# The first layer's mixer in two token halves, the second placed among the retrieval's slots

## Chip, cores and metric

The kernel runs on one core of one Trainium2 chip. The metric is the device time of one execution in microseconds (us). The kernel before has a median of 3397.39 us in 3 runs (3396.7 to 3400.4).

## What is computed

A decoder trunk of two layers on 512 tokens of 1,024 channels, all in 32-bit floats. Each layer is a mixer and then a channel mixer (PEER), both on normed rows and added to the residual. The first layer's mixer is a gated spatial mixing (gMLP, 4 groups, chunks of 128 tokens) beside an attention of 8 heads with compressed, selected and window branches; since at most 8 blocks of keys exist and the top 16 are asked for, the selected branch sees all causal keys, and so does the window of 512. The second layer's mixer is a gated linear recurrence (HGRN2, 8 heads). PEER takes most of the data:

```python
def even_mixer(h, w_in, ...):
    u, v, q, kc, vc, ks, vs, kw, vw, gt = jnp.split(h @ w_in, EVEN_SPLITS, axis=-1)
    a = chunked_gmlp(jax.nn.gelu(u), jax.nn.gelu(v), a_ln_w, a_ws, a_bs)
    b = nsa(q, kc, vc, ks, vs, kw, vw, gt, cmp_pos, ...)   # o = g0*o_cmp + g1*o_slc + g2*o_win
    return jnp.concatenate([a, b], axis=-1) @ w_out

def peer_block(xb):                       # 128 tokens
    s = scores of xb @ w_q against 2 x 128 keys, 8 heads
    best, pos = top 16 of the 16 x 16 sums of the two top-16 lists
    gate = softmax(best)
    act = gelu(einsum('td,thkd->thk', xb, u_tab[experts]))
    return einsum('thk,thkd->td', gate * act, v_tab[experts])
```

Each token thus needs 8 heads x 16 experts = 128 rows of the table of u and v, 8 KB each.

## The kernel before

Tokens are cut into 4 blocks of 128, one token to a partition. A **slot** is one gather: for the 128 tokens of a block, one expert row each, 128 x 8 KB = 1 MB. There are 1,024 slots: layer, block, head, rank. Eight buffers (`gath`, in `region_g`) hold gathered rows. In each slot GpSimd issues the gather (L568) once the row of eight slots ago is freed, VectorE takes the product of u with the normed row (L1153), ScalarE gelu, gate and a diagonal of the weights (`weigh`, L773 to L780), and TensorE adds diagonal times v to the block's sum (`row_product`, L1566), two 512-column products; each such 32-bit product is two instructions in the trace. In a few slots of phases 1 and 2 (`DVE_ROWS`) VectorE adds the row instead (L1162). Slots form four phases of 256 (`PHASE`): two blocks of one layer each.

All other work is generators of pieces, each with a tick (a slot number). Each engine's program is written out in one order: before or after slot s it issues all pieces whose tick has come. So an engine that waits in a piece holds the row work behind it.

- Before slot 0 stands the first layer's mixer for all four blocks, not in pieces: norm, transposes, feature products for q, k, v with 512 token columns (L1238), token-major products (L1251), compression of keys and values (L1265 for positions, L1271), gMLP, and attention in four rounds (`for c in range(0, 4)`) of 8 units, a unit being one block of queries and one of two heads: scores (L1310), bias and maximum on VectorE (L886, L888), exponentials (L640), transposes (L1338), copy (L655), values (L1348), then a combination of three branches on VectorE (L902 to L904). Last `project_out` (L1362) and the routing of the first two blocks (`routing_pieces`: norm, transposes, query products L1400, key scores L1413, then rankings on VectorE).
- Phase 0 (slots 0 to 255) holds the rest of routing job 0 and routing job 1 (blocks 2 and 3), one head in 13 to 14 slots. Phases 1 and 2 hold half of the recurrence each (`recurrence_pieces`, head every 19 slots) and a routing job, one head in 7 slots. Phase 3 holds no mixer.
- SyncE loads weights as **slabs** of about 1 MB into a ring of three (`slabs`). Slab i is issued when the user of slab i - 3 is done; the order is fixed. A routing slab has 1 KB pieces and 128 KB of keys. Slabs and gathers share the 16 transfer engines from different queues.
- The first gather waits for the routing of the first unit and for `wo_done` of all four blocks, as the weights of the output stand where gathered rows go.

## Time and profile before

| | |
|---|---|
| median of 3 runs | 3397.39 us |
| the profiled execution | 3394.91 us |
| its span | 3392.7 us |
| mean granted TensorE clock | 0.932 of 2.4 GHz |
| TensorE, VectorE, ScalarE, GpSimd busy | 2912.1, 2225.1, 1450.8, 1272.0 us |
| moved | 1178.72 MB, mean 347 GB/s |

The times of engines are sums over their instructions; a matmul's record includes its drain, and records overlap. In the profile's lines a row is a group of instructions: line, engine, operation, tile written <- tiles read, shapes, count, and then busy time with the mean of one, and the idle time before them with what ended it. A window's row gives the stretch, its length, then for PE (TensorE), PEld (its weight loads), DVE (VectorE), ACT (ScalarE) and POOL (GpSimd) the busy time with the count of instructions, then the granted clock, the share of the transfer engines, and GB/s. SPq and POOLq stand for the issue of transfers.

### The profile page before, as it was taken

To read this page: it belongs to the slowest core of one execution; us is meant where nothing else is said; L and a number is where in the kernel's file an instruction comes from. 1 tells how busy PE (TensorE), PEld (TensorE's weight loads), DVE (VectorE), ACT (ScalarE), POOL (GpSimd) and SP (SyncE) were. 2 spreads that over 40 slices of the span, in tenths; PEclk is the share of its full clock that TensorE was granted. 3 is DMA by queue.
4 is the path that set the end of the run, shared out by engine and by line. 5 is a ranking of instruction groups with operands and counts; after the bars stand their busy time and mean duration, and the time that the engine had idled before them with its cause. 6 is when DMAs were issued, how large, how long until landed. Compare 5 with 4: busy or idle time off the path is not lost.

```text
span 3392.7 us, 30594 instructions
## 1 busy us (share of the span) xinstructions
PE 2912.1 (86%) x8568; PEld 1544.7 (46%) x8568; DVE 2225.1 (66%) x5636; ACT 1450.8 (43%) x3950; POOL 1272.0 (37%) x1254
## 2 busy tenths in 40 slices
PE   7988888887898879898998978988989887787787
PEld 3655655442344435555545545555545532222222
DVE  1134415666766677888886678888886676667664
ACT  0022212444444446555544346555644444444443
POOL 2000003343443444444444344545454344444442
PEclk9865579999999999999999999999999999999999
DMA  4110007999999999999999999999999999999997
GB/s 169 63 42 0 1 7 304 415 415 419 396 414 414 421 411 415 377 376 382 390 401 412 412 411 420 369 387 383 391 403 412 410 417 422 421 421 406 422 421 325
DMA packets 198202, 1178.72 MB, mean 347 GB/s; under 512 B 20368, under 2 KB 57488, under 8 KB 61456
## 3 DMA queue, kind: packets, MB, share of 16 engines
q0 software_dynamic: 147456, 1073.81, 77.6%
q1 hardware_dynamic: 50576, 102.96, 8.1%
q8 instruction: 68, 1.11, 0.1%
q14 instruction: 102, 0.84, 0.1%
HBM read 1173.55 MB, written 2.10 MB: 347 GB/s over the span
## 4 chain that ended last, share of the span: by engine, by line
PE 44%; DMA 29%; DVE 13%; ACT 7%; issue 4%; POOL 2%; SPq 0%; DVEq 0%; POOLq 0%; ACTq 0%
DMA region_g<-in_uv_dram,experts 26%; PE ps L1566 20%; DVE region_g L1153 6%; PE ps L1400 5%; DMA region_a<-in_keys_dram 3%; PE ps L1437 2%; PE ps L1348 2%; PE ps L1251 2%; PE ps L1310 2%; PE ps L1362 2%; PE ps L1238 2%; POOL region_g L568 1%; PE ps L1338 1%; ACT x_res L780 1%; PE ps L1434 1%
## 5 line engine op out<-in xcount | busy, mean ns | idle before, releaser
L1566 PE MATMUL ps<-region_g,x_res 128*128 128x512 f32 x3840 | 1875.4, 621 | 333.0 <-ACT x_res L780 303.3
L568 POOL DMA_INDIRECT region_g<-in_uv_dram,experts x1024 | 1142.2, 1115 | 1614.7 <-PE ps L1566 1355.5
L1153 DVE CUSTOM_DVE_ANT_0 region_g<-region_g,region_h 128x1024 f32<-128x1024 f32 x1024 | 1255.2, 1228 | 579.5 <-DMA region_g<-in_uv_dram,experts 568.5
L1566 PEld LDWEIGHTS ps<-region_g,x_res 128*128 128x128 f32 x3840 | 706.5, 195 | 1249.9 <-ACT x_res L780 622.1
L773 ACT ACTIVATE region_a<-region_a 128x1 f32<-128x1 f32 x1024 | 207.0, 202 | 1360.2 <-DVE region_a L1153 1357.0
L780 ACT ACTIVATE x_res<-ident_z,region_a 128x128 f32<-128x128 f32 x960 | 385.4, 401 | 31.4
L774 ACT ACTIVATE region_a<-region_a,gate 128x1 f32<-128x1 f32 x1024 | 301.5, 294 | 33.3
L1400 PE MATMUL ps<-region_a 128*128 128x256 f32 x1024 | 243.7, 383 | 8.5 <-DMA region_a<-in_keys_dram 7.3
L1400 PEld LDWEIGHTS ps<-region_a 128*128 128x128 f32 x1024 | 196.5, 192 | 86.2 <-issue 55.1
L773 ACT ACT_TABLE_LOAD x110 | 141.1, 1283 | 6.8 <-DVE region_a L1153 4.9
L1434 PE MATMUL ps<-region_a 128*128 128x256 f32 x512 | 133.3, 391 | 1.0 <-DVE region_a L993 1.0
L1434 PEld LDWEIGHTS ps<-region_a 128*128 128x128 f32 x512 | 101.9, 200 | 66.1 <-issue 57.6
L1437 PE MATMUL ps<-region_a 128*128 128x256 f32 x512 | 129.1, 379 | 0.0
L1437 PEld LDWEIGHTS ps<-region_a 128*128 128x128 f32 x512 | 96.7, 190 | 58.0 <-issue 50.7
L520 POOL TENSOR_SCALAR rst<-rst 128x1 f32<-128x1 f32 x8 | 1.8, 226 | 312.9 <-ACT region_h L681 312.4
L1348 PEld LDWEIGHTS ps<-region_c 128*128 128x128 f32 x320 | 70.6, 328 | 38.0 <-issue 25.8
L902 DVE TENSOR_SCALAR region_c<-ps,coef 128x64 f32<-128x64 f32 x32 | 9.1, 283 | 115.8 <-PE ps L1351 115.8
L1153 DVE DVE_READ_ACCUMULATOR2_ANT region_a<- 128x1 f32 x1024 | 84.6, 83 | 0.0
L1348 PE MATMUL ps<-region_c 128*128 128x64 f32 x320 | 76.6, 426 | 8.9 <-ACT region_c L655 8.9
L1162 DVE SCALAR_TENSOR_TENSOR x_res<-region_g,region_a,x_res 128x1024 f32<-128x1024 f32 x64 | 82.0, 1281 | 0.0
L765 ACT ACT_TABLE_LOAD x63 | 80.8, 1283 | 1.1
L1310 PE MATMUL ps<-region_c 64*128 64x128 f32 (+3 forms) x128 | 74.6, 767 | 0.0
(221 smaller groups left out, 2469.9 us busy)
## 6 DMA issues: line engine op xcount, KB each, us to landing
region_a<-in_w_q_dram SPq DMA_DIRECT2D x32, 1024.0 KB
region_a<-in_w_odd_dram SPq DMA_DIRECT2D x32, 1024.0 KB
region_g<-in_uv_dram,experts POOLq DMA_INDIRECT x1024
region_a<-in_w_out_o_dram SPq DMA_DIRECT2D x8, 1024.0 KB
region_a<-in_w_even_dram SPq DMA_DIRECT2D x1, 5216.0 KB, 19.9
region_a<-in_w_even_dram SPq DMA_DIRECT2D x1, 4096.0 KB, 16.4
region_g<-in_w_out_e_dram SPq DMA_DIRECT2D x1, 4096.0 KB, 13.5
region_a<-in_keys_dram SPq DMA_DIRECT2D x32, 128.0 KB
```

The costliest lines, as they stand in the source:

```text
L568: g.indirect_dma_start(out=gath[:, s % NBUF, :], out_offset=None, in_=uv[s // (2 * PHASE)], in_offset=bass.IndirectOffsetOnAxis(ap=experts ...
L773: link(a.activation(gact[:, c:c + 1], dots[:, c:c + 1], ACT.Gelu_apprx_tanh))
L774: i = a.activation(wts[:, c:c + 1], gact[:, c:c + 1], ACT.Copy, scale=gate[:, n % 2, k:k + 1])
L780: a.activation(diag[:, pe_n(s) % NBUF, :], ident, ACT.Copy, scale=wts[:, c:c + 1]).then_inc(diag_ready.sem, 1)
L1153: v.tensor_tensor_reduce(out=u_, in0=u_, in1=XNr[n // P_HEADS % 3], scale=1.0, scalar=0.0, op0=ALU.mult, op1=ALU.add, accum_out=dots[:, c: ...
L1162: v.scalar_tensor_tensor(xb, gath[:, s % NBUF, D_MODEL:ROW], wts[:, c:c + 1], xb, ALU.mult, ALU.add).then_inc(vd_done.sem, 1)
L1310: k_ = t.matmul(PS[:, 2 * par + br, 0:nk], qst[r, qb * P:(qb + 1) * P], kT[r, br, 0:nk], start=True, stop=True)
L1348: t.matmul(PS[:, 6 + par, br * HD:(br + 1) * HD], pTs[:, par, br * SEQ + kt * P:br * SEQ + (kt + 1) * P], vsw[:, kt, br, e * HD:(e + 1) * ...
L1400: i = t.matmul(PS[:, 4 + h % 2, p * HALF:(p + 1) * HALF], W[:, c, p * P:(p + 1) * P], hTh[:, c, :], start=c == 0, stop=c == KC - 1)
L1434: i = t.matmul(PS[:, 2, o * HALF:(o + 1) * HALF], W[:, c % 4, o * P:(o + 1) * P], hTh[:, c, :], start=c == 0, stop=c == KC - 1)
L1437: i = t.matmul(PS[:, 3, o * HALF:(o + 1) * HALF], hTh[:, c, o * P:(o + 1) * P], W[:, c % 4, HALF:2 * HALF], start=c == 0, stop=c == KC - 1)
L1566: i = t.matmul(PS[:, j, :], diag[:, pe_n(s) % NBUF, :], gath[:, s % NBUF, D_MODEL + j * 512:D_MODEL + (j + 1) * 512], start=first, stop=last)
```

## The change

The first layer's mixer is written as pieces and runs twice, for blocks 0 and 1 (`even_pieces(0)`) ahead of all slots (`EVEN_AT[0]` is -1000), and for blocks 2 and 3 (`even_pieces(1)`) from slot 0 of phase 0. Its ticks: norm 0 to 12, feature products 12 to 44, the 280 columns of v and gates 44 to 52, compression 52 to 68, value channels 68 to 84, gate channels 84 to 100, attention 102 to 170 in 16 units of four ticks (`ATT`, `UNITS`), output 150 to 178. Products have 256 token columns instead of 512; all weights of this mixer are loaded once for each half. Keys and values of the first half are kept for the second. `Threads` merges mixer and routing by tick. Routing job 1 goes from slot 130 and a head per 13 slots to slot 182 and a head per 7.

The attention's unit changes: exponentials in place, then coefficients (gate over sum) on VectorE and a scaling of the probabilities on ScalarE, then transposes of one branch at a time through one bank; value products have the values as weights and two heads' probabilities as 256 moving columns, so that all branches add up in one sum that comes out transposed. The combination on VectorE and the output transposes are gone. The compressed probabilities are weighed for all heads of a half at once. Scores have one pair of banks instead of two.

Weights of the first half have a ring of seven slabs in `region_g`; those of the second go through the ring of three, merged by tick with the routing slabs. The first gather waits for the output of the first half. Copies of positions in pairs (`positions_in_pairs`) are issued by SyncE in the slab order, 8 for the first half and 16 for the second; the position vector is a third plane of the compression's moving operand. In phase 0 VectorE adds two of 16 rows, as in phases 1 and 2. Level masks (the recurrence's) are built by GpSimd in phase 0 rather than at the start. Routing uses one bank for queries and one for scores instead of two each.

```diff
...
+UNITS = 16
+ATT = 102
...
-DVE_ROWS = ((), (5, 13), (5, 13), ())
+EVEN_AT = (-1000, 0)
+DVE_ROWS = ((5, 13), (5, 13), (5, 13), ())
...
+        class Threads:
+            def __init__(self, *gens):
+                self.gens = [[next(g), g] for g in gens]
+            def run(self, tick):
+                while True:
+                    due = [t for t in self.gens if t[0] is not None and t[0] <= tick]
+                    if not due:
+                        return
+                    first = min(due, key=lambda t: t[0])
+                    first[0] = next(first[1], None)
         NORM_AT = HEADS_AT + 7 * HEAD_PACE + 30
-        NORM_TICK = (-100, 130, PHASE + NORM_AT, 2 * PHASE + NORM_AT)
+        NORM_TICK = (-100, ATT + 80, PHASE + NORM_AT, 2 * PHASE + NORM_AT)
...
+        def even_slabs(q):
+            t = EVEN_AT[q]
+            out_ = [(t + 12 + 8 * i, ("F", q, i), (f_done, 4 * q + i)) for i in range(4)]
+            out_ += [(t + 44, ("G", q), (g_done, q))]
+            out_ += [(t + 52 + 8 * kv, ("C", q, kv), ((c_half, q), (hid_done, q))[kv]) for kv in range(2)]
+            out_ += [(t + 68 + 8 * i, ("V", q, i), ((v_half, q), (v_done, 2 * q + 1))[i]) for i in range(2)]
+            out_ += [(t + 84 + 8 * i, ("U", q, i), ((u_half, q), (u_done, 2 * q + 1))[i]) for i in range(2)]
+            return out_ + output_slabs(q, t + ATT + 48)
+        def output_slabs(o, t):
+            return [(t + 4 * j, ("O", o, j), (pw_used, 3 * o + j) if j < 3 else (pw_done, 4 * o + 3)) for j in range(4)]
...
+        first_order = even_slabs(0)
+        order_ = even_slabs(1) + routing_slabs(0) + routing_slabs(1)
         for q_ in range(2):
...
+            def positions_in_pairs(q):
+                sp.wait_ge(f_out.sem, f_out.at(4 * q + 3))
+                for kv in range(2):
+                    for g in range(2):
+                        own = slice(g * HD, (g + 1) * HD)
+                        src, dst = kvc[own, kv, :], dup[:, kv, g, :]
+                        sp.dma_start(dst[0:HD, CMP_STRIDE:WIDE], src).then_inc(dup_in, 16)
+                        sp.dma_start(dst[HD:P, CMP_STRIDE - 1:WIDE - 1], src).then_inc(dup_in, 16)
+                        if q:
+                            sp.dma_start(dst[0:HD, 0:CMP_STRIDE], kvl[own, kv, :]).then_inc(dup_in, 16)
+                            sp.dma_start(dst[HD:P, 0:CMP_STRIDE - 1], kvl[own, kv, 1:CMP_STRIDE]).then_inc(dup_in, 16)
...
+            for i in range(7, len(first_order)):
+                first_slab(i)
+            for i in range(3, len(order_)):
+                if order_[i][1] == ("C", 1, 0):
+                    positions_in_pairs(1)
+                if order_[i][1] == ("H", 0, 0, 0):
+                    sp.wait_ge(r_xn.sem, r_xn.at(3))
+                    sp.dma_start(wrow, w_ffn[1:2, :].partition_broadcast(P)).then_inc(ffn_in, 16)
+                slab(i)
...
+            pool.wait_ge(pw_done.sem, pw_done.at(3))
...
+                for step in range(2, 4 * UNITS + 8, 2):
+                    yield t0 + ATT + step
+                    if step == 4:
+                        gated_out(q, 1)
+                    if step % 4 == 0:
+                        if step >= 8:
+                            probabilities_out(q, step // 4 - 2, 1)
+                        if step // 4 <= UNITS:
+                            scaled(q, step // 4 - 1)
+                    else:
+                        if step >= 22 and step % 16 == 6:
+                            heads_out(q, (step - 22) // 16)
+                        if 6 <= step and (step - 6) // 4 < UNITS:
+                            probabilities_out(q, (step - 6) // 4, 0)
+                        if step // 4 < UNITS:
+                            exponentials(q, step // 4)
...
+            def exponentials(q, u):
+                n, par = UNITS * q + u, u % 2
+                nk = (2 * q + unit(u)[1] + 1) * P
+                act.wait_ge(z_ready.sem, z_ready.at(n))
+                for br in range(2):
+                    last = a.activation(zs[:, par, br, 0:nk], zs[:, par, br, 0:nk], ACT.Exp, bias=nmax[:, par, br:br + 1],
+                                        scale=0.125, accum_out=sums[:, par, br:br + 1])
+                last.then_inc(p_ready.sem, 1)
+            def scaled(q, u):
+                n, par = UNITS * q + u, u % 2
+                nk = (2 * q + unit(u)[1] + 1) * P
+                act.wait_ge(coef_ready.sem, coef_ready.at(n))
+                for br in range(2):
+                    last = a.activation(zs[:, par, br, 0:nk], zs[:, par, br, 0:nk], ACT.Copy, scale=coef[:, par, br:br + 1])
+                last.then_inc(ps_ready.sem, 1)
+            def probabilities_out(q, u, br):
+                n = UNITS * q + u
+                nt = 2 * q + unit(u)[1] + 1
+                act.wait_ge(pT_done.sem, pT_done.at(2 * n + br))
+                after(act, pv_done, n // 2 - 1)
+                last = a.activation(pT[:, br, 0:nt, u % 2 * P:(u % 2 + 1) * P], v3(PS[:, 6, 0:nt * P], nt), ACT.Copy)
...
+                for step in range(2, 4 * UNITS + 2, 2):
+                    yield t0 + ATT + step
+                    if step % 4 == 0:
+                        coefficients(q, step // 4 - 1)
+                    else:
+                        biased(q, step // 4)
+            def biased(q, u):
+                n, par = UNITS * q + u, u % 2
+                pair, t, e, c = unit(u)
+                nk = (2 * q + t + 1) * P
+                dve.wait_ge(sc_done.sem, sc_done.at(n))
+                after(dve, pT_done, 2 * (n - 2) + 1)
+                z = zs[:, par, :, 0:nk]
+                link(v.scalar_tensor_tensor(z, bmid(alibi[:, SEQ - nk:SEQ], 2), slope8(head_of(e, 2 * pair + c)),
+                                            PS[:, 2:4, 0:nk], ALU.mult, ALU.add))
+                link(v.tensor_reduce(nmax[:, par, :], z, AXX, ALU.max))
+                v.tensor_scalar(nmax[:, par, :], nmax[:, par, :], -0.125, None, ALU.mult).then_inc(z_ready.sem, 1)
+            def coefficients(q, u):
+                n, par = UNITS * q + u, u % 2
+                pair, t, e, c = unit(u)
+                h = head_of(e, 2 * pair + c)
+                dve.wait_ge(p_ready.sem, p_ready.at(n))
+                link(v.reciprocal(coef[:, par, :], sums[:, par, :]))
+                v.tensor_tensor(coef[:, par, :], coef[:, par, :], gates[:, 2 * q + t, 3 * h + 1:3 * h + 3], ALU.mult
+                                ).then_inc(coef_ready.sem, 1)
...
+                start, wins, planes = ((CMP_STRIDE, 15, 3), (0, 16, 2))[q]
...
+                for step in range(4, 4 * UNITS + 8, 2):
+                    yield t0 + ATT + step
+                    u = step // 4
+                    if step % 4 == 0:
+                        if u < UNITS:
+                            scores(q, u)
+                        if step >= 12 and u % 2 == 1:
+                            values(q, u - 2)
+                        if 1 <= u <= UNITS:
+                            probability_transposes(q, u - 1, 0)
+                    elif step >= 6 and u - 1 < UNITS:
+                        probability_transposes(q, u - 1, 1)
+                        if (u - 1) % 2 == 1:
+                            compressed_transposes(q, u - 1)
+                    for x_ in range(2):
+                        out_step = step - 48 + x_
+                        if 0 <= out_step < 12 and out_step % 2 == 0:
+                            output_piece(q, out_step // 4, 2 + out_step // 2 % 2)
+                for x_ in range(6):
+                    yield t0 + ATT + 68 + (x_ + 1) // 2
+                    output_piece(q, x_ // 2, x_ % 2)
+                for bank in range(4):
+                    yield t0 + ATT + 72 + bank
+                    output_piece(q, 3, bank)
...
+            def scores(q, u):
+                n = UNITS * q + u
+                pair, r, e, c = unit(u)
+                nk, own = (2 * q + r + 1) * P, slice(e * HD, (e + 1) * HD)
+                if u:
+                    pe.wait_ge(z_ready.sem, z_ready.at(n - 1))
+                else:
+                    pe.wait_ge(u_out.sem, u_out.at(2 * q + 1))
+                for br in range(2):
+                    i = t.matmul(PS[:, 2 + br, 0:nk], qT[own, 2 * pair + c, r * P:(r + 1) * P], kT[own, br, 0:nk],
                                  start=True, stop=True)
-                i.then_inc(mix_done.sem, 1)
-                if tb + 1 < TB:
...
+                after(pe, pT_out, 2 * n + br - 1)
+                for kt in range(2 * q + r + 1):
+                    i = t.transpose(PS[:, 6, kt * P:(kt + 1) * P], zs[:, u % 2, br, kt * P:(kt + 1) * P], ident)
...
+            def values(q, u):
+                n = UNITS * q + u
+                pair, r, e, _ = unit(u)
+                own = slice(e * HD, (e + 1) * HD)
+                pe.wait_ge(pT_out.sem, pT_out.at(2 * n + 1))
+                pe.wait_ge(pcT_out.sem, pcT_out.at(n // 2))
+                if e == 0:
+                    after(pe, pv_out, n // 4 - 1)
+                for br in range(2):
+                    for kt in range(2 * q + r + 1):
+                        t.matmul(PS[own, 7, 0:HALF], vsw[:, kt, br, own], pT[:, br, kt, :],
+                                 start=br == 0 and kt == 0, stop=False)
+                t.matmul(PS[own, 7, 0:HALF], vcmp[:, own], pcT, start=False, stop=True).then_inc(pv_done.sem, 1)
...
-                            after(pe, r_qo, n - 2)
-                            if job >= 2 and h < 2:
-                                after(pe, res_out, 4 * (job - 2) + 2 + h)
+                            if h:
+                                after(pe, r_qo, n - 1)
+                            else:
...
-                    if h >= 2 or job == 1:
-                        after(pe, scored, n - 2)
...
+                        after(pe, scored, n - 1)
...
```

## Rows read from the trace of the kernel before

**Rows 1.** The page's 40 slices, transfer engines and rate

```profile
DMA  4110007999999999999999999999999999999997
GB/s 169 63 42 0 1 7 304 415 415 419 396 414 414 421 411 415 377 376 382 390 401 412 412 411 420 369 387 383 391 403 412 410 417 422 421 421 406 422 421 325
```

**Rows 2.** Windows by stage of before; columns as told above

```profile
29.00:200.00 171.00, 163.22 (x536) 94.95 (x535) 26.85 (x61) 21.84 (x45) 8.40 (x12) 0.91 0.20 72
200.00:453.00 253.00, 222.58 (x753) 158.67 (x752) 106.84 (x293) 68.17 (x169) 0.00 (x0) 0.50 0.01 3
453.00:531.00 78.00, 70.90 (x190) 36.21 (x189) 15.18 (x45) 6.42 (x11) 1.60 (x4) 0.92 0.07 22
543.00:1240.00 697.00, 592.25 (x1600) 288.15 (x1600) 452.66 (x1153) 298.22 (x877) 278.82 (x260) 0.98 1.01 414
1240.00:1994.00 754.00, 670.43 (x2192) 385.42 (x2192) 586.66 (x1494) 389.67 (x1011) 342.79 (x336) 0.96 0.99 397
1994.00:2738.00 744.00, 665.29 (x2208) 385.81 (x2208) 582.03 (x1481) 388.61 (x1007) 349.41 (x336) 0.97 0.99 397
2738.00:3392.00 654.00, 511.48 (x1024) 182.40 (x1024) 436.63 (x1077) 276.66 (x830) 262.86 (x256) 0.97 0.98 407
```

**Rows 3.** Timeline, first gather, first dot product, block sum of slot 258

```profile
531.02 1.25 POOL L568 DMA_INDIRECT region_g<-in_uv_dram,experts  x1 [29.27 <-PE ps L1362]
543.21 1.23 DVE L1153 CUSTOM_DVE_ANT_0 region_g<-region_g,region_h 128x1024 f32<-128x1024 f32 x1 [0.18 <-DVE region_c L1081]
...
1239.50 1.22 DVE L1170 TENSOR_TENSOR x_res<-x_res,ps 128x1024 f32<-128x1024 f32 x1
```

**Rows 4.** Timeline, TensorE: start, duration, runs of instructions

```profile
103.79 10.77 PE L1265 MATMUL ps<-pos_sb,region_g 128*128 128x1 f32 x64
114.41 13.89 PE L1271 MATMUL ps<-region_g 128*128 128x62 f32 x64
...
497.65 1.04 PE L1369 MATMUL ps<-ident_z,region_h 128*128 128x128 f32 x8
516.81 13.90 PE L1362 MATMUL ps<-region_g 128*128 128x512 f32 x32
530.54 7.07 PE L1400 MATMUL ps<-region_a 128*128 128x256 f32 x32
```

**Rows 5.** Chain of waits, pieces in order of time: start, duration

```profile
28.66 56.78 PE ps L1238 x128
267.66 2.00 PE ps L1310 x4
...
289.89 3.71 PE ps L1310 x4
...
1899.63 45.15 DMA region_a<-in_keys_dram
```

**Rows 6.** Groups by form, 200 to 453 us, attention

```profile
L640 ACT ACTIVATE region_h<-region_h,nmax 128x512 f32<-128x512 f32 x16 | 11.4, 714 | 11.6 <-DVEq L890 11.6
L886 DVE SCALAR_TENSOR_TENSOR region_h<-alibi,slope,ps 128x1024 f32<-128x1024 f32 x8 | 10.3, 1281 | 1.8 <-DVE region_c L904 1.8
L888 DVE TENSOR_REDUCE nmax<-region_h 128x2 f32<-128x1024 f32 x8 | 9.8, 1220 | 0.3
```

**Rows 7.** Timeline, ScalarE in phase 1, a table load

```profile
1409.56 1.28 ACT L732 ACT_TABLE_LOAD   x1
1410.85 0.42 ACT L732 ACTIVATE region_a<-region_a 128x256 f32<-128x256 f32 x1
```

**Rows 8.** Timeline, TensorE: first query products of two routing heads

```profile
1902.28 1.89 PE L1400 MATMUL ps<-region_a 128*128 128x256 f32 x8
...
1922.48 1.89 PE L1400 MATMUL ps<-region_a 128*128 128x256 f32 x8
```

**Rows 9.** The page's transfer queues: gathers, then slabs

```profile
q0 software_dynamic: 147456, 1073.81, 77.6%
q1 hardware_dynamic: 50576, 102.96, 8.1%
```

1255 lines of the change are left out of this document (631 added, 624 removed).

## Prediction

> **What bounds the kernel now.** I read the slices of the page first: the transfer engines are idle early and full from the seventh slice on [rows 1]. The windows by stage [rows 2] divide the execution in two. Up to 531 us the first layer's mixer runs alone, bound by TensorE or by chains of waits; its attention (200 to 453) has a granted clock of 0.50, the 1.2 GHz level, throughout. From the first gather at 531.02 [rows 3] the 1,024 gathers of 1 MB rule: transfer share 0.97 to 1.01, 397 to 414 GB/s. So time can come from two places: the first 531 us, in which nothing is gathered, and bytes or stalls in the four phases of 256 slots behind. Phase 0 ends, with the block sum of slot 258, at 1239.50 [rows 3], 708.5 us after the first gather. Phases 1 and 2, which already have a mixer woven in, take 754 and 744 us by their windows; phase 3 has none and takes about 645. Phase 0 has only routing woven in, and TensorE is busy 592 of 697 us [rows 2], drains of products included; its work itself I count below.
>
> **Part 1, the time before the first gather.** The change does blocks 0 and 1 only. First products start at 28.66 with four blocks normed [rows 5]; with two, and the chain square, root, scale, transposes, copy on two blocks, I take 16. Feature products: 128 instructions of 512 columns took 56.78 [rows 5]; at 256 columns 32 instructions take 7.07 [rows 4], so 128 take 28. The 280-column products 8. The eight copies of k and v rows must be issued and land: 3 beyond that cover. Compression is bound by loading weights, 64 instructions in 13.89 [rows 4], and doesn't halve: 14. The position products (10.77 [rows 4]) ride in it and go. Value and gate channels, 64 products of 256 columns, 28. Compressed scores, mixing, transposes and the waits for the layer norm: 12. Attention then starts at 109, against about 200.
> Its 16 units (two blocks, 8 heads) see 128 or 256 keys. In the chain of before the four units of the two lower blocks take 289.89 - 267.66 = 22.2 us of each round [rows 5], four rounds 89. The new unit drops the three-step combining and adds a coefficient step and two scalings between exponentials and transposes, with one score buffer instead of two: at the low clock I work out 5.6 us at 256 keys, 4.3 at 128, so 80 (69 if all were 4.3; 89 as before). Six output pieces inside add 10.4 at the high clock and 21 at the low one; I take 15. End at 204. Behind it: ten output pieces at 1.74 (16 products, 32 instructions, 13.90 [rows 4], so 0.87 each), 18.2 with the last addition; then norm, routing head 0 and ranking of the first unit 29: the window of 78 us before the first gather [rows 2] less three blocks' output, 48 products at 0.91 in that window, and less some 5 us by which the fourth block's output delayed that gather. **First gather at 251**, so 280 us earlier (260 to 300: the unit bounds, and the clock of the tail).
>
> **Part 2, phase 0 with blocks 2 and 3 woven in.** TensorE, at the high clock, from [rows 4]: row products now 256 x 1.74 = 445 plus 14 routing heads x 8 = 112, together 561. After: 32 rows go to VectorE (-55); added are features 28, the 280-column products 8, compression 14, value and gate 28, scores 24 (16 of 384 and 16 of 512 columns), 128 transposes at 0.13 = 17, values and compressed values 64 x 0.44 = 28, output 32 x 0.87 = 28, small ones 9. Sum 184; 690 in all. Phase 1 by the same count: 386 rows, projections 110, levels 28, output 28, routing 62, rest 28 = 642, and it takes 754.
> Transfers: 268 MB of gathers and 16.5 of routing slabs stay; 15.9 MB of weights, formerly loaded while nothing was gathered, come on top: 301 MB. At 414 GB/s 727 us, at phase 1's 397 758 [rows 2]. So the weaving isn't free even at best: the weights alone cost 38 us.
> By stretches:
> - First transfers to first dot: 12, as 531.02 to 543.21 [rows 3].
> - Slots 0 to 101. TensorE 1.52 for a row and 1.35 of mixer and routing, 2.87 a slot; transfers 126 MB, 305 us. Sixteen slabs must pass here. Under gathers the routing slabs of phase 1, at 7 slots' pace, follow each other at 1922.48 - 1902.28 = 20.2 us [rows 8], and one took 45 from issue to landing, mostly queued [rows 5]. A slab of 1 KB pieces is 64 turns an engine, with keys 80: 0.25 us a turn. The new order needs about 1,136 turns, 287 us, in some 90 slots, and bunches them (three slabs in slots 28 to 36). TensorE waits for some, with row products queued behind in its order, and those hold gather buffers. 325 (305 to 360).
> - Attention, 64 slots, 16 units. Per unit of 4 slots TensorE has 11.1. ScalarE: 4 x 1.09 (phase 3's busy time a slot [rows 2]) = 4.4; two exponentials with reads 1.5 at 512 keys (0.71 each [rows 6]); scalings 1.2, copies 1.2, shares of others 0.3; two table loads 2.57, since each unit goes from gelu to exp and back [rows 7]: 11.2, 10.6 at 384 keys. It also stands in the exponentials until VectorE has done bias and maximum, 1.28 + 1.22 + 0.17 [rows 6], about 1.2 beyond its own work, with `weigh` of the next slots queued behind; on those wait TensorE, then the gather issue. VectorE: 4 x 1.72 (phase 3 again) + 3.0 + 0.6 = 10.5. Three engines at 10.5 to 12 with a crosswise order: 13 a unit, 208 (179 if only ScalarE's work counts; 256 at 16, if each unit's waits add up).
> - Slots 166 to 181: 14 rows 24, ten output pieces 17, a wait for the last slab: 45.
> - Slots 182 to 257, routing 1 at 7 slots a head, as in phases 1 and 2 (2.9 a slot): 220.
> **Phase 0 takes 810**, 101 more than now (750 to 880).
>
> **Part 3, the rest.** From 1239.50 to the end, 2153 us: slots, ticks and rows on VectorE stay. Routing loses its second banks for queries and scores; each copy is due two slots or more before the bank's next user, so I price it at 0; if that cover fails, eight heads x about 1 us in two phases, 15. Level masks (23 small GpSimd instructions) move from the start into phase 0, between gather issues of 0.94 us, under transfers: 0, or up to 5 if an issue is late.
>
> **Rules of the Trainium skill beside this.** "DMA: Bandwidth & Descriptors", section on queues, rings and completion order, says that an engine takes turns between rows of queues packet by packet. Taken as one record of each, a turn is 0.286 + 0.087 = 0.373 us from the queue shares [rows 9], the 1,136 turns 424 us instead of 325, and the total 3318; rows 8 show 0.25 a turn, so one for one is too dear, and the page itself lets several descriptors pass in one packet. "ScalarE: Activation LUTs", what a table load costs, has 1.28 us plus a drain of 1.38. In 16 units x 2 that would be 44 more, 3263; rows 7 show the next activation 1.29 after the load's start, without a drain.
>
> **The sum.** 251 + 810 + 2153 = 3214 of span, against 3392.7. The profiled execution took 3394.9, 2.2 beyond its span: 3216; the median of the runs is 2.5 above it: **3219**.
>
> **The rivals.**
> - A, transfers alone decide: phase 0 like phase 1, 758 + 12. Then 3179. For it: the share of 0.97 to 1.01 with a mixer woven in, and 8 buffers that cover a late engine. Against: 48 us more TensorE work than phase 1, and ScalarE near full in the attention. 0.20.
> - B, the attention's order binds: 16 us a unit and waits for slabs at 360: +48 + 35, 3302. For it: table loads per unit and three steps between engines at slot grain. Against: buffers. 0.17.
> - C, one turn per record for the slabs: 3318, as above. 0.04.
> - D, the weight slabs queue one behind the other. If each of the 15 slabs due by slot 92 needs its own 45 us [rows 5] before the next is on its way, the first 102 slots take some 700 instead of 325 and the total is 3594, slower than before. It decides from 178 us over my 325, that is at about 31 us a slab. Against: two are in flight at once and 20.2 is the spacing seen, in a stretch where both queues are full [rows 8]. 0.04.
> - E, it doesn't do what it says: the gathers still wait for work of the second half. Then the first gather stays near 531 and only bytes are added, 3397 + 38 = 3435. The first gather waits for the first half's output alone, so 0.02.
> The forecast has the rest, 0.53.
>
> **How the numbers follow.** Around 3219: first part -20/+20, slots 0 to 101 -20/+35, attention -29/+48, the rest -8/+25. All good ends together give 3142, all bad ones 3347. Rivals A, B and C lie inside, D and E are left out (0.06), and a little beyond either end: the range is 3142 to 3345. About 0.2% (7 us) is what a measurement of this kernel can tell from no change. Faster: the forecast, A, B and C and nearly nothing against them, 0.93; same 0.01; slower, D and E, 0.06.
>
> **What would show it.** First gather near 251, at 230 with a high clock in the attention, above 280 if units don't shorten. Attention's low clock again. In phase 0: gathered GB/s near 372 over 810 us; TensorE waiting for slab transfers in slots 16 to 92, absent now; a unit period of 13 us, ScalarE above 90% busy there with some 32 more table loads; VectorE below. If the second layer's phases move by over 1%, part 3 is wrong. The forecast fails most easily if the slab queue starves (a stretch of slots 20 to 92 above 3.6 us a slot) or doesn't matter at all (2.9).

## The result, and the profile after

The changed kernel takes 3190.11 us (median of 4 runs, 3186.6 to 3192.3), the kernel before 3397.5 beside it: a ratio of 0.9387, 95% interval [0.9371, 0.9403]. The forecast was 3219 in a range of 3142 to 3345. The profiled execution took 3188.19 us, with a span of 3186.2 and a mean granted clock of 0.951.

The page's slices, each a fortieth of the span, answer [rows 1]. The transfers' gap now ends in the fourth slice instead of the seventh. Behind it two dips to 331 and 337 GB/s are new, in slices 9 and 10, which is the attention of blocks 2 and 3:

```profile
DMA  7009899988999999999999999999999999999997
GB/s 278 14 1 368 346 367 385 413 331 337 404 419 422 425 392 385 391 374 386 406 420 418 420 417 387 362 395 384 401 417 419 409 426 427 427 425 414 427 427 330
```

The windows by stage answer [rows 2]; columns as there. The stretches are: the norm; products to gates; attention of blocks 0 and 1; its tail; then, in slots of phase 0, slots 0 to 31, 32 to 87, 88 to 103, 104 to 167 with attention, 168 to the block sum; phases 1, 2, 3:

```profile
0.00:16.00 16.00, 3.70 (x16) 3.14 (x16) 2.92 (x5) 5.88 (x7) 4.59 (x18) 1.00 0.95 309
16.00:102.00 86.00, 82.07 (x388) 71.14 (x388) 14.52 (x34) 11.59 (x23) 3.81 (x5) 0.90 0.59 212
102.00:197.00 95.00, 81.36 (x247) 42.79 (x245) 27.55 (x88) 42.91 (x144) 0.00 (x0) 0.69 0.00 1
197.00:251.00 54.00, 40.95 (x138) 26.63 (x136) 14.68 (x49) 7.40 (x13) 1.79 (x5) 0.84 0.07 22
251.00:345.00 94.00, 82.58 (x280) 51.54 (x280) 64.93 (x163) 40.97 (x113) 47.48 (x41) 0.91 1.02 417
345.00:551.00 206.00, 171.65 (x630) 110.58 (x629) 116.24 (x282) 71.92 (x202) 61.74 (x60) 0.92 0.93 358
551.00:594.00 43.00, 39.17 (x131) 22.22 (x129) 34.35 (x86) 17.88 (x53) 20.86 (x17) 1.00 1.01 427
594.00:791.00 197.00, 178.31 (x532) 81.24 (x532) 162.79 (x375) 158.61 (x365) 85.42 (x87) 0.97 0.90 348
791.00:1052.00 261.00, 234.75 (x720) 130.10 (x720) 173.63 (x418) 107.03 (x313) 109.08 (x96) 0.97 1.02 415
1052.00:1800.00 748.00, 670.82 (x2192) 386.25 (x2192) 586.80 (x1494) 390.32 (x1012) 344.99 (x336) 0.96 0.99 401
1800.00:2541.00 741.00, 666.84 (x2208) 386.66 (x2208) 582.19 (x1481) 388.54 (x1007) 351.24 (x336) 0.97 0.99 399
2541.00:3186.00 645.00, 510.38 (x1024) 183.23 (x1024) 436.98 (x1077) 276.63 (x830) 260.13 (x256) 0.97 0.98 413
```

The timeline's first gather, first dot product and block sum of slot 258 answer [rows 3]:

```profile
250.81 1.25 POOL L635 DMA_INDIRECT region_g<-in_uv_dram,experts  x1 [26.86 <-DVE gate L1220]
258.77 1.23 DVE L1255 CUSTOM_DVE_ANT_0 region_g<-region_g,region_h 128x1024 f32<-128x1024 f32 x1 [5.45 <-DMA region_g<-in_uv_dram,experts]
...
1051.71 1.22 DVE L1272 TENSOR_TENSOR x_res<-x_res,ps 128x1024 f32<-128x1024 f32 x1
```

So the first gather comes 280.2 us earlier, phase 0 takes 800.9 us instead of 708.5, and from the block sum to the end it is 2134.5 instead of 2153.2: -280.2 + 92.4 - 18.7 = -206.5, the whole difference of the two spans.

The chain of waits in order of time (start, duration, what) shows what is new in phase 0. Before, no slab stood on the chain in this phase; now four do, each the keys of a routing head. Three lie in slots 0 to 101, 31 to 34 us from the start of the issue to landing. The fourth, 47.79 us, stands near the end of the phase, where the heads follow each other every 7 slots as in phases 1 and 2, whose chain has such a row too, before ([rows 5], 45.15) as after:

```profile
325.19 34.26 DMA region_a<-in_keys_dram
...
382.52 31.44 DMA region_a<-in_keys_dram
...
471.32 32.59 DMA region_a<-in_keys_dram
...
956.75 47.79 DMA region_a<-in_keys_dram
```

The timeline of TensorE for the first of them gives the wait in brackets, and that of SyncE's queue the issues: the query columns (L439) are issued at 324.61, and the issue of the keys (L442) is itself held for 10.00 us, since the queue still has other slabs of small pieces in it:

```profile
359.50 3.78 PE L1575 MATMUL ps<-region_a 128*128 128x256 f32 x8 [14.27 <-DMA region_a<-in_keys_dram]
...
324.61 0.54 SPq L439 DMA_DIRECT2D region_a<-in_w_q_dram  x1
325.19 10.00 SPq L442 DMA_DIRECT2D region_a<-in_keys_dram  x1
```

That the queue's earlier slabs are what holds the issue is read from the order of the rows; runs 1 and 3 below bear on it by the size of the pieces.

In what follows, "us a slot" is the distance of dot products divided by the slots between them. In the changed kernel: slots 0 to 31 2.69, 32 to 87 **3.69**, 88 to 103 2.69, 104 to 167 3.07, 168 to 255 2.90; before, 2.67, 2.74, 2.54, 2.67, 2.72.

### The profile page after: what moved, and what is told of

The parts are those of the page before. It is cut to its first block, busy times and chain, and to the rows that moved or that the text cites. A ratio compares the mean times of both kernels' runs of the same rounds, so it can differ in the third digit from the quotient of the medians.

```text
span 3186.2 us, 30486 instructions
## 1 busy us (share of the span) xinstructions
PE 2762.6 (87%) x8496; PEld 1495.5 (47%) x8496; DVE 2217.6 (70%) x5544; ACT 1519.7 (48%) x4079; POOL 1291.1 (41%) x1254
## 4 chain that ended last, share of the span: by engine, by line
PE 45%; DMA 25%; DVE 13%; ACT 10%; issue 4%; POOL 2%; SPq 1%; POOLq 0%; DVEq 0%; ACTq 0%
PE ps L1745 23%; DMA region_g<-in_uv_dram,experts 18%; DMA region_a<-in_keys_dram 8%; DVE region_g L1255 6%; PE ps L1575 5%; PE ps L1607 3%; PE ps L1636 2%; PE ps L1539 1%; PE ps L1339 1%; ACT L882 1%; ACT x_res L889 1%; POOL region_g L635 1%; PE ps L1604 1%; PE ps L1653 1%; PE ps L1499 1%
## 5 line engine op out<-in xcount | busy, mean ns | idle before, releaser
L1745 PE MATMUL ps<-region_g,x_res 128*128 128x512 f32 x3712 | 1813.2, 621 | 260.6 <-ACT x_res L889 229.4
L635 POOL DMA_INDIRECT region_g<-in_uv_dram,experts x1024 | 1168.3, 1141 | 1645.3 <-PE ps L1745 1344.5
L1745 PEld LDWEIGHTS ps<-region_g,x_res 128*128 128x128 f32 x3712 | 690.7, 196 | 1089.9 <-issue 571.1
L882 ACT ACTIVATE region_a<-region_a 128x1 f32<-128x1 f32 x1024 | 206.0, 201 | 1245.3 <-DVE region_a L1255 1238.8
L889 ACT ACTIVATE x_res<-ident,region_a 128x128 f32<-128x128 f32 x928 | 372.6, 402 | 30.3
L883 ACT ACTIVATE region_a<-region_a,gate 128x1 f32<-128x1 f32 x1024 | 301.6, 295 | 33.3
L1575 PE MATMUL ps<-region_a 128*128 128x256 f32 x1024 | 253.7, 395 | 49.9 <-DMA region_a<-in_keys_dram 48.7
L1575 PEld LDWEIGHTS ps<-region_a 128*128 128x128 f32 x1024 | 201.2, 198 | 125.5 <-DMA region_a<-in_keys_dram 54.9
L1604 PE MATMUL ps<-region_a 128*128 128x256 f32 x512 | 135.7, 396 | 1.0 <-DVE region_a L1091 1.0
L1604 PEld LDWEIGHTS ps<-region_a 128*128 128x128 f32 x512 | 102.9, 202 | 67.1 <-issue 58.2
L1264 DVE SCALAR_TENSOR_TENSOR x_res<-region_g,region_a,x_res 128x1024 f32<-128x1024 f32 x96 | 123.2, 1283 | 10.9 <-ACT region_a L883 5.6
L1607 PE MATMUL ps<-region_a 128*128 128x256 f32 x512 | 129.1, 379 | 0.0
L1607 PEld LDWEIGHTS ps<-region_a 128*128 128x128 f32 x512 | 96.7, 190 | 58.0 <-issue 50.7
L1636 PE MATMUL ps<-region_a 128*128 128x512 f32 x192 | 88.9, 593 | 0.0
L1653 PEld LDWEIGHTS ps<-region_a 128*128 128x128 f32 x512 | 66.4, 191 | 12.3 <-POOL region_a L601 6.9
L1653 PE MATMUL ps<-region_a 128*128 128x128 f32 x512 | 67.8, 276 | 4.5 <-POOL region_a L601 4.3
L1067 DVE COPY_PREDICATED region_a<-level_mask,ps 128x256 f32<-128x256 int32 x128 | 56.6, 442 | 20.7 <-PE ps L1653 11.3
```

What stands on the lines that cost most here:

```text
L635: g.indirect_dma_start(out=gath[:, s % NBUF, :], out_offset=None, in_=uv[s // (2 * PHASE)], in_offset=bass.IndirectOffsetOnAxis(ap=experts ...
L882: link(a.activation(gact[:, c:c + 1], dots[:, c:c + 1], ACT.Gelu_apprx_tanh))
L883: i = a.activation(wts[:, c:c + 1], gact[:, c:c + 1], ACT.Copy, scale=gate[:, n % 2, k:k + 1])
L889: a.activation(diag[:, pe_n(s) % NBUF, :], ident, ACT.Copy, scale=wts[:, c:c + 1]).then_inc(diag_ready.sem, 1)
L1264: v.scalar_tensor_tensor(xb, gath[:, s % NBUF, D_MODEL:ROW], wts[:, c:c + 1], xb, ALU.mult, ALU.add).then_inc(vd_done.sem, 1)
L1575: i = t.matmul(PS[:, 4, p * HALF:(p + 1) * HALF], W[:, c, p * P:(p + 1) * P], hTh[:, c, :], start=c == 0, stop=c == KC - 1)
```

## The experiments

Theory S: what phase 0 lost beyond its bytes and its attention was lost to slabs, in slots 32 to 87, and by the shape of their pieces. Rival W: this stretch is bound by TensorE's work. Run 1, run 2 and so on mean the numbered sections below. Further questions were what weaving itself is worth, what binds the attention, and where the 18.7 us came from that phases 1 to 3 gained without having been changed.

### 1. Mixer slabs in wide pieces

All slabs of the first layer's mixer that came as eight pieces of 1 KB a partition come as one piece of 8 KB; routing slabs stay.

```diff
-                    return w_even[:, :, lo:lo + HALF]
+                    return w_even[i]
...
-                    return w_even[:, :, 512 + i * HALF:512 + (i + 1) * HALF]
+                    return w_even[4 + i]
...
-                    return w_even[:, :, i * HALF:(i + 1) * HALF]
+                    return w_even[6 + i]
```

> The changed kernel with the nine slabs F, G, V, U of each half laid out so that a partition's part is one contiguous piece of 8 KB (G 8.75 KB) instead of eight of 1 KB. Bytes, order and ring are as in the changed kernel (3190). Theory S, the slab queue starves under gathers because it moves piece by piece: slots 32 to 88, now 3.69 us each, fall to about 2.9, TensorE no longer waits 33 us for slabs there, total 3150 (3140 to 3165). Rival W, it is bytes and TensorE's work that fill these slots: 3185 or more.

Measured: 3184.39 us (3180.3 to 3185.2), ratio 0.9374 [0.9359, 0.9390]; slots 32 to 87 at 3.57 instead of 3.69. S is not borne out by these slabs. But the waits are still there, in TensorE's table of waits for this stretch (in total, times, longest), first of the changed kernel, then of this run: shorter, and four instead of three.

```profile
PE ps L1575 <- DMA region_a<-in_keys_dram: 32.8, 3, 14.3
...
PE ps L1574 <- DMA region_a<-in_keys_dram: 28.1, 4, 7.6
```

All are for routing slabs, which this run left in small pieces. What did go is the hold on SyncE: the issue of the same keys takes 0.66 us instead of 10.00, and none of the four in slots 0 to 101 takes over 0.77.

```profile
322.77 0.66 SPq L441 DMA_DIRECT2D region_a<-in_keys_dram  x1
```

So it was the mixer's small pieces that held the issue there, and the hold cost little: without it the keys still take 22 to 28 us from issue to landing on this run's chain, and 28.1 of 32.8 us of waits are left.

### 2. All slabs in wide pieces

The routing slabs too: a head's query columns and keys as one piece of 9 KB a partition and one transfer.

```diff
-                return w_q[name[1] // 2][:, :, i * HALF:(i + 1) * HALF]
+                return w_q[name[1] // 2][i]
...
-                if name[0] == "R":
-                    _, job, h = name
-                    sp.dma_start(dst[:, KC * HALF:SLAB].rearrange("p (a b) -> p a b", a=2),
-                                 keys[job // 2][:, 2 * h:2 * h + 2, :]).then_inc(there, 16)
```

> As the kernel with wide mixer slabs, and the routing slabs too in one contiguous piece a partition, keys included (9 KB, one transfer instead of two). Theory S: the routing stages of phases 0 to 2 had the slab queue full at 20.2 us a slab, so they gain as well, a few us each; total 10 to 25 below the kernel with wide mixer slabs, near 3130. Rival W: no more than 3 below it, as only bytes count.

Measured: 3146.32 us (3144.2 to 3149.2), ratio 0.9262 [0.9247, 0.9278], 44 below the changed kernel and 38 below run 1. Slots 32 to 87 take 3.09 us. Its window over them:

```profile
346.00:519.00 173.00, 165.90 (x621) 107.62 (x620) 116.72 (x283) 72.50 (x202) 65.79 (x59) 0.96 1.01 417
```

This row against 345:551 above is the reading: 56 slots in 173 us instead of 206, transfer share 1.01 instead of 0.93, 417 GB/s instead of 358, and the same work of TensorE (166 against 172 us busy, at a clock of 0.96 against 0.92). The stretch had been neither full of transfers nor full of products; it waited in a chain from slab to products to row products to gather buffers.

### 3. Routing slabs alone, and keys apart

Which slabs, and what in them: the second transfer, or the pieces? One run has only the routing slabs wide (the diff of run 2, without that of run 1); the other has everything wide, but the keys again as a transfer of their own, of 512-byte pieces.

> Only the routing slabs are laid out anew: query columns and keys of a head come as one piece of 9 KB per partition instead of eight of 1 KB and two of 512 bytes in a second transfer; all slabs of the two mixers stay as in the changed kernel. If the routing slabs alone are the cause of the 14 us waits (all ten of the long waits of TensorE in phase 0 named the keys' transfer), slots 32 to 88 take 3.1 us each as with all slabs wide (3.69 in the changed kernel), and the total is 3146 to 3155. If the pieces of the mixers' slabs count equally once the routing slabs are mended, it lands between, at 3160 to 3175.

> As with all slabs wide, but the keys of a head are again a second transfer of two 512-byte pieces per partition, and the query columns one piece of 8 KB. Theory K: what TensorE waited for was the second transfer, queued behind the first in the same queue, so most of the 38 us come back: 3170 to 3185, waits again named after the keys. Rival N: the number of pieces counts (16 turns of an engine for the keys against 64 for the 1 KB pieces of the columns), so a fifth of the 38 us comes back: 3150 to 3156, slots 32 to 88 at 3.1 to 3.2 us.

Measured: routing slabs alone 3151.08 us (3146.8 to 3152.6), ratio 0.9276 [0.9260, 0.9291], slots 32 to 87 at 3.13. Keys apart 3150.74 us (3150.0 to 3151.3), 0.9279 [0.9264, 0.9295], 3.08.

So 39 of the 44 us hang on the routing slabs. From run 1 to the run with the keys apart nothing changes but the pieces of the query columns, 1 KB to 8 KB, and the time falls by 33.6 us (3184.39 to 3150.74): that much is these pieces alone. The keys' second transfer is the 4.4 us between this run and run 2, whose intervals overlap, so its worth isn't settled; theory K, that most of the 38 us is the second transfer, falls. No issue of keys takes over 0.43 us in slots 0 to 101 here. The new layout also makes a whole slab one stretch of memory in HBM; that it is the length of the pieces and not this was not tested.

The trace of the changed kernel named the keys because they land last, not because they were the cause. In the run with the routing slabs alone the waits of TensorE for slabs in phase 0 are down to one for a mixer slab and one for a routing slab:

```profile
PE ps L1344 <- DMA region_a<-in_w_even_dram: 3.4, 1, 3.4
...
PE ps L1571 <- DMA region_a<-in_w_q_dram: 2.3, 1, 2.3
```

Why small pieces hurt in routing slabs and hardly in the mixer's is only argued: routing heads 2 to 7 are due at every 14th slot whatever the slab queue holds, and their slabs stand behind up to two others of the ring of three.

### 4. The compression's slab ahead of the row copies

In run 2 one wait for a slab was left in slots 32 to 87, 7.1 us for the first compression slab. SyncE issued it at 393.42, behind sixteen copies of key and value rows that took it from 383.31 to 393.4. I moved the copies in two ways: ahead of the second compression slab, and directly behind the first.

```diff
-                if order_[i][1] == ("C", 1, 0):
+                if order_[i][1] == ("C", 1, 1):
                     positions_in_pairs(1)
```

> All slabs wide, and SyncE issues the load of the first compression slab ahead of its sixteen copies of key and value rows instead of behind them (the wait for the fourth feature product stands ahead of the copies). The last wait of TensorE for weights between 250 and 700 us, 7.1 us at 417.7 for that slab, should go: 3139, 7 less than with the slabs alone. If TensorE then waits for the copies, which can't start earlier, or buffers of the gathers cover the 7 us, the total stays within 3 of 3146.

Measured: 3156.96 us (3155.9 to 3168.1), ratio 0.9308 [0.9287, 0.9329], 11 *above* run 2. TensorE's compression row shows a wait of 16.79 us, put down to nothing that the profile shows, and the rows of SyncE's queue say why (the first copy is L461, the last L465):

```profile
379.88 0.33 SPq L438 DMA_DIRECT2D region_a<-in_ck_dram  x1
407.24 0.33 SPq L438 DMA_DIRECT2D region_a<-in_w_q_dram  x1
407.61 0.47 SPq L461 DMA_DIRECT2D region_a<-region_h  x1
...
417.07 0.60 SPq L465 DMA_DIRECT2D region_a<-kvl  x1
...
427.43 1.89 PE L1357 MATMUL ps<-region_a 128*128 128x32 f32 x8 [16.79 <-issue]
```

Between the two compression slabs stands a routing slab in SyncE's order, whose load waits for its buffer until 407.24. I had moved sixteen copies past that wait without looking. The second way puts them ahead of it:

```diff
                 slab(i)
+                if order_[i][1] == ("C", 1, 0):
+                    positions_in_pairs(1)
```

> All slabs wide, the sixteen row copies directly behind the load of the first compression slab. In the run with that load ahead of the copies, the copies had also moved behind the next routing slab's load, whose wait for its buffer held SyncE until 407.24, so they were issued at 407.6 to 417.7 instead of 383.3 to 393.4, and the compression waited 16.8 us. Now they go out at about 383.7. If that is the whole story, the first block of 128 slots falls from 389.5 us to 383 (7.1 us of wait gone) and the total is 3139. If the eight gather buffers cover that wait, 389 and 3146.

Measured: 3143.88 us (3140.3 to 3148.8), ratio 0.9251 [0.9236, 0.9267]; from the first gather to the first block sum it takes 386.6 us instead of 389.5. The slab is no longer waited for, the copies are:

```profile
PE ps L1357 <- DMA region_a<-kvl: 3.6, 1, 3.6
```

Of 7.1 us half was turned into another wait. The totals of runs 2 and 4 overlap; that it is faster than run 2 isn't shown, though it has the lowest median of all. It is 46 us under the changed kernel and some 254 under the one before.

### 5. No weaving

The second half of the mixer is also done before all slots (with the new attention and 256 columns), so nothing of it is woven in. Beside the line shown, five waits of TensorE follow the new order.

```diff
-        EVEN_AT = (-1000, 0)
+        EVEN_AT = (-1000, -500)
```

> The changed kernel with the second half's mixer also ahead of all slots, behind the first's: two halves and the new attention, but no weaving. The second half alone takes about 90 to its attention and 125 in it and its output, so the first gather comes near 251 + 215 = 466; phase 0 falls back to 700 or a little below, as VectorE has two of 16 rows. Total 466 + 700 + 2134 = 3300, so weaving is worth 110 and the two halves with the new attention about 97. Rival, the new form is worth nothing and all comes from weaving: 3390.

Measured: 3329.11 us (3328.4 to 3330.4), ratio 0.9801 [0.9784, 0.9817]. Its first gather:

```profile
492.35 1.25 POOL L635 DMA_INDIRECT region_g<-in_uv_dram,experts  x1 [26.01 <-DVE gate L1220]
```

The second half takes 492.35 - 250.81 = 241.5 us when it stands alone, and phase 0 then 695.3. Woven in it lengthens phase 0 by 800.9 - 695.3 = 105.6 us. **Weaving is worth 139 us** (3329.11 - 3190.11), two thirds of the change's gain; the new form of the mixer by itself brings the first gather from 531.02 to 492.35, 38.7 us.

### 6. No rows on VectorE in phase 0

```diff
-DVE_ROWS = ((5, 13), (5, 13), (5, 13), ())
+DVE_ROWS = ((), (5, 13), (5, 13), ())
```

> The changed kernel with no rows on VectorE in phase 0, so 32 rows or 55 us of work go back to TensorE. If TensorE binds the attention's slots, those 8 rows there and some before cost their work, total 3210 to 3225. If ScalarE or the transfers bind, 3190 within 5, or a little less since VectorE is relieved of 41 us.

Measured: 3199.85 us (3182.0 to 3203.8), ratio 0.9407 [0.9375, 0.9440]. The interval overlaps that of the changed kernel, so a difference of 10 us isn't settled. In the profiled executions phase 0 takes 801.3 us against 800.9, and 8.0 of the 9.7 us between the two spans stand behind it, where the programs are the same. The 55 us of TensorE's work that the rows take away were not on the path: the attention's slots take 3.05 with and 3.07 without the extra load, and slots 32 to 87 3.61 and 3.69.

### 7. Attention without table loads

For blocks 2 and 3 the exponentials are replaced by the identity, with the same shapes and accumulations, so the kernel leaves out the exponentials there and nothing else. It takes away ScalarE's change of tables at every unit.

```diff
-                    last = a.activation(zs[:, par, br, 0:nk], zs[:, par, br, 0:nk], ACT.Exp, bias=nmax[:, par, br:br + 1],
+                    last = a.activation(zs[:, par, br, 0:nk], zs[:, par, br, 0:nk], ACT.Identity if q else ACT.Exp, bias=nmax[:, par, br:br + 1],
```

> The changed kernel with the exponentials of blocks 2 and 3 replaced by a linear function that every table holds. Its output is therefore another one; all else is done as before. It takes 32 table loads of 1.28 us, 41 us, from ScalarE in the 64 slots of the woven attention. Theory ScalarE binds there: its slots fall from 3.07 to some 2.7 us each, total 3165. Rival, TensorE (11.1 a unit) and the order between engines bind: the slots stay over 2.95, total 3183 to 3190.

Measured: 3177.38 us (3173.3 to 3179.6), ratio 0.9355 [0.9339, 0.9371]. ScalarE's groups in the changed kernel's attention, 594 to 791 us:

```profile
L882 ACT ACT_TABLE_LOAD x20 | 25.7, 1283 | 0.3
L889 ACT ACTIVATE x_res<-ident,region_a 128x128 f32<-128x128 f32 x55 | 22.1, 402 | 1.8
...
L740 ACT ACT_TABLE_LOAD x16 | 20.5, 1283 | 0.3
...
L883 ACT ACTIVATE region_a<-region_a,gate 128x1 f32<-128x1 f32 x63 | 18.6, 295 | 2.0
...
L882 ACT ACTIVATE region_a<-region_a 128x1 f32<-128x1 f32 x63 | 12.2, 193 | 5.4 <-DVE region_a L1255 5.2
...
L874 ACT ACT_TABLE_LOAD x4 | 5.1, 1283 | 0.1
```

These are 40 loads, 51.3 us. In the run's window eight are left, four at L882 and four at L874, 10.2 us, so 32 or 41 us are gone, and its 64 slots take 15 us less (3.07 to 2.84 a slot). Its window over them, 182 us:

```profile
590.00:772.00 182.00, 173.21 (x529) 80.46 (x530) 160.49 (x374) 116.95 (x331) 88.32 (x85) 0.99 0.95 379
```

ScalarE falls from 158.61 of 197 us (81%) to 116.95 of 182 (64%); TensorE rises from 91% to 95%, VectorE from 83% to 88%. So ScalarE was one of two: relieved of a quarter of its work, the attention gives back a third of that, and by these shares it is TensorE that it meets then.

### 8. The kernel before, with its buffers moved

Phases 1 to 3 gained 18.7 us though neither slots nor order changed there. What did change is that `region_a`, which lies ahead of the gather buffers in SBUF, is 640 bytes a partition longer. So: the kernel before, with that length and nothing else.

```diff
-        RA = sb("region_a", [P, KC * W_EVEN])
+        RA = sb("region_a", [P, 18784])
```

> The kernel before with its first region 640 bytes a partition longer, as the changed kernel has it, so that gather buffers lie at the changed kernel's places; nothing else. In the changed kernel phase 3, whose work is the same, took 9.7 us less, and phases 1 and 2 9 less together. Theory P, the place of the buffers sets the transfers' pace: 3378 to 3382. Rival, it is something else: 3397 within 3.

Measured: 3375.04 us (3367.4 to 3376.5), ratio 0.9927 [0.9910, 0.9945]. **22 us of the change's 207 come from where the buffers lie**, as priced in the kernel before. The page's slices of this run, against the second line of [rows 1], show it where gathers run alone: 427 instead of 421 and 422 GB/s in the last tenth.

```profile
GB/s 170 63 42 0 1 6 276 422 423 425 394 422 421 426 415 407 379 374 394 377 403 420 419 423 416 373 382 383 380 408 420 414 411 427 427 427 417 427 427 338
```

In a stretch of phase 3 with gathers alone the gather queue fills the engines' time in both kernels, 100.7% of 3080:3360 before and 100.5% of 3060:3340 in this run, with 16,094 and 16,262 packets: a packet of a gather takes 0.280 us before and 0.277 here.

Which places are good? Two runs with all slabs wide (the second with the order of run 4) put the buffers elsewhere, 640 bytes further and 128 bytes further than the changed kernel has them:

```diff
-        RA = sb("region_a", [P, 18784])
+        RA = sb("region_a", [P, 18944])
```

> All slabs wide, and the region ahead of the gather buffers is 640 bytes per partition longer, so that the buffers lie on a multiple of 2048 bytes (75,776 instead of 75,136 bytes from the first region's start). Nothing else differs. If what a buffer's place gives is a matter of alignment to 2 KB, blocks of 128 gathers without a mixer (319.8 us before, 315.0 with the place moved) change again, by 5 us or more either way, and the total by 20 or more. If any place but the one before serves as well, 3146 within 5.

> As the kernel with the copies behind the compression slab's load, and the gather buffers 128 bytes further along the partition: 75,264 bytes from the first region's start. So far 74,496 and 75,776 bytes (582 and 592 times 128) gave 325 and 319.5 us for the last two blocks of 128 gathers, and 75,136 (587 times 128) gave 320.8 and 315.0. If the good places are those off a multiple of 256 bytes, this one (588 times 128) gives 325 and 319.5 again and a total 20 to 26 above the kernel it is compared with. If the place matters in some coarser way (near 75,136 good, 640 bytes off bad), it gives 321 and 315 and no difference.

Measured: 3172.19 us (3168.3 to 3174.4), ratio 0.9344 [0.9329, 0.9360], and 3171.70 us (3167.5 to 3176.9), 0.9339 [0.9323, 0.9355]: 26 and 28 above the same kernels at the changed kernel's place. The slices of the first; those of the second are within 2 GB/s of them from slice 32 to 39:

```profile
GB/s 279 14 1 364 419 406 413 405 328 343 417 421 421 418 381 385 383 389 389 410 421 421 419 417 362 387 390 375 406 420 421 415 422 421 422 405 418 421 422 320
```

The last two blocks of 128 gathers, from block sum to block sum:

| bytes ahead of the buffers, a partition | in units of 128 | last two blocks, us |
|---|---|---|
| 74,496 (before) | 582 | 325.3, 319.8 |
| 75,136 (after, and before with its buffers moved) | 587 | 320.6, 314.9; 319.8, 315.1 |
| 75,264 | 588 | 325.2, 319.1 |
| 75,776 | 592 | 325.3, 319.2 |

Three places on a multiple of 256 bytes give one value, the place off it another, and there is nothing between. The other nine runs have the changed kernel's place, and their blocks take 320.1 to 320.9 and 314.6 to 315.4. One good place is few: that it is the odd multiple of 128 that does it fits all four and was foretold for 588, but no second odd one was run. The places are counted from the start of `region_a`; whether that start lies on a multiple of 256 bytes itself no run here shows, so which kind of place is the aligned one by address stays open. Everything that lies behind the buffers moved with them, so that it is the buffers' own place is argued from the gathers' rate and packets, not separated.

## Why the prediction was right, and where not

| step | forecast, us | measured, us |
|---|---|---|
| attention of blocks 0 and 1 starts | 109 | 108.5 |
| it ends, with six output pieces | 204 | 197.2 |
| tail to the first gather | 47 | 53.6 |
| **first gather** | **251** | **250.8** |
| to the first dot product | 12 | 8.0 |
| slots 0 to 101 | 325 | 330.2 |
| attention, 64 slots | 208 | 195.8 |
| slots 166 to 181 | 45 | 53.2 |
| slots 182 to 257 and the sum | 220 | 213.7 |
| **phase 0** | **810** | **800.9** |
| **the rest** | **2153** | **2134.5** |
| span | 3214 | 3186.2 |

**The head** came out to the microsecond, partly by two errors that cancel. The attention with its output pieces took 88.8 us where I had 95: its granted clock of 0.69 wasn't the 0.50 of [rows 2] throughout; while the six output pieces ran (165 to 183) it was 0.87. The tail took 7 more than worked out, at a clock of 0.84 against 0.92 in the same window before. The first 109 us, products at the high clock sized from [rows 4] and [rows 5], were right within 1.

**Slots 0 to 101** were right in sum and in mechanism: the forecast put 20 us on waits for slabs there, TensorE waiting and row products behind it holding the buffers. The signs that it named are in the trace (3.69 us a slot in slots 32 to 87, against the 3.6 given as the mark of a starving queue). Its price came from [rows 8], 20.2 us a slab, and from turns of 1 KB pieces; runs 1 to 3 show that pieces decide, and that it is the routing slabs'. With slabs wide, these slots take 302 us, near the 305 that the forecast gave as the transfers' own. Rival D, slabs in series, decides from 31 us a slab; three did take 31 to 34 from issue to landing, but they overlapped with others: SyncE issued 14 slabs between 284.74 and 529.00, under 19 us apart. Rival C, a turn of 0.373 us a piece, would have made the stretch 424: not so.

**The attention** took 12.2 us a unit, not 13. ScalarE was busy 158.61 / 16 = 9.9 a unit, not 10.6 to 11.2, so 81% where the forecast named over 90% as the sign, and VectorE, named as below it, 83%. The term that was too high is `weigh`, 4.4 for four slots. Its three groups (L889, L883, L882 in the rows of run 7) are 22.1 + 18.6 + 12.2 = 52.9 us, 3.3 a unit: phase 3's busy time, from which I took it, holds that phase's own table loads too, and rows that go to VectorE don't pass the 128x128 step. Run 7 shows that neither ScalarE alone nor the crosswise order alone binds. Rival B, 16 a unit, falls. The 40 table loads of this window took 1.283 us each, and beside ScalarE's busy time its 197 us have room for 38 in all. The Trainium skill, "ScalarE: Activation LUTs", what a table load costs, gives 1.28 us and a drain of 1.38. The load agrees; 40 such drains would be an estimated 55 us, for which there is no room: not borne out here.

**Slots 166 to 181** took 8 more. TensorE is the bound there, busy 50.67 of 53 us:

```profile
785.00:838.00 53.00, 50.67 (x137) 23.28 (x136) 32.49 (x80) 23.63 (x65) 20.78 (x18) 1.00 0.95 362
```

I had counted 14 rows and ten output pieces; the window has 65 records of row products, so 16 rows, two more at 1.74 us each, and the last units' values and transposes, 6.6 us of products, still had to pass.

**Rival A** (transfers alone, 3179) was nearer to the median than the forecast, and yet wrong as a mechanism: it wants phase 0 in 770 us, which took 801, and came near only because the rest, which it leaves as it was, fell by 18.7. With slabs wide, phase 0 is 767 us and the total 3146: then its phase 0 holds, the attention's 0.90 of transfer share apart.

**The rest** is the step that failed: priced at 0 with -8/+25, measured -18.7. By the forecast's own mark, phases that move by over 1%, part 3 was wrong: phase 3 fell from 654 to 645 us by its window, 1.4%. I had looked for costs in what executes there (banks, level masks) and found none, rightly; the layout of SBUF, which the change also altered, stood in the diff and I gave it no term. Run 8 prices it: 13.5 us in phases 1 to 3 (block sums 2130.3 us apart instead of 2143.8) and 8.7 in phase 0. The other 5 of the 18.7 lie in phases 1 and 2 and are within what kernels at one place scatter by: these two phases together take 1488.6 to 1497.6 us in the changed kernel, the one before with its buffers moved, and runs 1, 5, 6 and 7.

Two slips change nothing above: TensorE's 445 + 112 in phase 0 is 557 and not 561, and the upper end of the range, 3345, is 2 us inside the sum of all bad ends and not beyond it.

So the 207 us are: 139 from weaving, about 46 from the mixer's new form in two halves (38.7 of them before the first gather), 22 from the place of the buffers. The last is the price in the kernel before; with all slabs wide the place was worth 26 and 28.

## What to carry to other kernels

Work woven into a stretch that is bound by transfers still costs its bytes, here an estimated 38 us of 106 (15.9 MB at 414 GB/s). Where it needs slabs that stream in on the way, the form of their transfers can cost as much as the bytes: laying each head's routing weights out as one piece a partition gave 39 us without one more instruction. Before moving a transfer in a queue, list every issue that it passes, with what each waits for. And when a change alters the length of a buffer, compare a stretch in which nothing else changed: a difference there may be the layout's, and a run with that length alone prices it.

## What the runs showed of the hardware

- Gathers of 8 KB rows ran at 427 GB/s with their buffers (and all that lies behind them) at 75,136 bytes from the first region's start and at 421 to 422 at 74,496, 75,264 and 75,776: 1.2 to 1.4%, over 1,024 gathers 22 to 28 us.
- Beside gathers, three routing slabs of 1 KB pieces took 31 to 34 us from the issue of their last part to landing in slots 0 to 101, and one at 7 slots a head 47.79. The issue of the keys was held on SyncE for up to 10.00 us in slots 0 to 101 and for up to 20.30 at 7 slots a head; with the mixer's slabs in wide pieces it took 0.77 at most in slots 0 to 101, and landing came 22 to 28 us after. With all slabs in pieces of 8 or 9 KB TensorE didn't wait for a routing slab at all.
- The keys as a second transfer of 128 KB in 512-byte pieces, behind wide slabs, made a difference of 4.4 us over 32 heads, within overlapping intervals.
- TensorE's granted clock in the attention of blocks 0 and 1 was 0.63 from 102 to 165 us, where scores, transposes and values alternate with waits (52.7 of 63 us busy), so mostly the 1.2 GHz level, and 0.87 from 165 to 183 us, where output pieces stand between them and it is busy throughout.
